# A residual block with three MLPs: the norm's roots ahead of the last two MLPs taken per token column and spread by matmuls

## The reference

```python
def _rmsnorm(x, g):
    xf = x.astype(jnp.float32)
    y = xf * lax.rsqrt(jnp.mean(xf * xf, axis=-1, keepdims=True) + RMS_EPS)
    return (y * g.astype(jnp.float32)).astype(x.dtype)

def _sqrelu_mlp(h, w_up, w_down):
    a = jax.nn.relu(jnp.einsum('bld,df->blf', h, w_up))
    return jnp.einsum('blf,fd->bld', a * a, w_down)

    for i in range(DEPTH_2):
        ...
        h = _rmsnorm(hres, norm_g[i, 2])
        hres = hres + _rmsnorm(_sqrelu_mlp(h, w_up[i], w_down[i]), norm_g[i, 3])
```

## Time and profile before

| | |
|---|---|
| time, median of 3 runs | 2014.34 us (2013.67 to 2019.06) |
| the profiled execution | 2016.18 us, of it a span of 2014.4 us from first to last instruction |
| PE busy | 1916.4 us (95%) |
| DVE busy | 1278.6 us (63%) |
| ACT busy | 785.0 us (39%) |
| mean granted TensorE clock | 0.975 of full speed |

### The profile page before, as it was taken

The page is one execution under the profiler, slowest core; times in us unless marked ns, Lnnn a source line. Parts: engine busy times, 40 slices in busy tenths (PEclk is TensorE's granted clock), DMA queues, the critical chain, the costliest instruction groups (busy, mean ns, idle before and its releaser), DMA issues.

```text
span 2014.4 us, 28679 instructions
## 1 busy us (share of the span) xinstructions
PE 1916.4 (95%) x11702; PEld 1690.6 (84%) x11702; DVE 1278.6 (63%) x1912; ACT 785.0 (39%) x1180; POOL 156.3 (8%) x127
## 2 busy tenths in 40 slices
PE   7999899999999899999988999999899988999996
PEld 6876777888888778989888999999899866898995
DVE  7676646434434776766658677776655467777774
ACT  4555434222213343443334444443422244444441
POOL 3000033000000220000011000000300130000001
PEclk9999999999999999999998999999899988999998
DMA  5130121223232131111121233233122311332321
GB/s 178 63 105 21 53 84 63 101 88 105 84 105 104 64 104 63 43 43 43 64 81 46 84 105 105 84 106 105 54 93 85 105 63 63 105 105 86 107 101 42
DMA packets 26077, 166.44 MB, mean 83 GB/s; under 512 B 3808, under 2 KB 4064, under 8 KB 6624
## 3 DMA queue, kind: packets, MB, share of 16 engines
q1 hardware_dynamic: 25232, 163.52, 23.7%
q10 hardware_dynamic: 720, 1.14, 0.2%
HBM read 162.55 MB, written 2.10 MB: 82 GB/s over the span
## 4 chain that ended last, share of the span: by engine, by line
PE 42%; DVE 7%; ACT 1%; issue 1%; ACTq 0%; DVEq 0%
PE ps L2515 6%; PE ps L2516 6%; PE ps L2517 6%; PE ps L2531 4%; PE ps L2530 4%; PE ps L2529 4%; PE ps L372 3%; PE ps L374 3%; PE ps L373 3%; DVE ps L529 1%; DVE h L542 1%; DVE z_lo L480 1%; DVE w_lo L354 1%; ACT w_hi L343 0%; DVE arena L1885 0%
## 5 line engine op out<-in xcount | busy, mean ns | idle before, releaser
L372 PE MATMUL ps<-z_hi,w_hi 128*128 128x512 f32 (+1 forms) x1008 | 368.4, 365 | 30.6 <-DVE z_lo L480 27.5
L373 PE MATMUL ps<-z_lo,w_hi 128*128 128x512 f32 (+1 forms) x1008 | 364.3, 361 | 0.0
L374 PE MATMUL ps<-z_hi,w_lo 128*128 128x512 f32 (+1 forms) x1008 | 363.0, 360 | 0.0
L354 DVE TENSOR_TENSOR w_lo<-w_raw,w_hi 128x2048 fp32r<-128x2048 f32 x95 | 217.7, 2292 | 97.9 <-ACT w_hi L343 97.8
L2515 PE MATMUL ps<-arena,w_hi 128*128 128x256 f32 (+2 forms) x768 | 249.8, 325 | 17.6 <-DVE acc L1848 8.8
L372 PEld LDWEIGHTS ps<-z_hi,w_hi 128*128 128x128 f32 x1008 | 195.0, 193 | 67.9 <-issue 22.8
L2516 PE MATMUL ps<-arena,w_hi 128*128 128x256 f32 (+2 forms) x768 | 249.5, 325 | 0.0
L2517 PE MATMUL ps<-arena,w_lo 128*128 128x256 f32 (+2 forms) x768 | 248.9, 324 | 0.0
L343 ACT ACTIVATE w_hi<-w_raw 128x2048 fp32r<-128x2048 f32 x95 | 180.9, 1904 | 144.4 <-PE ps L374 131.6
L374 PEld LDWEIGHTS ps<-z_hi,w_lo 128*128 128x128 f32 x1008 | 194.8, 193 | 29.8
L373 PEld LDWEIGHTS ps<-z_lo,w_hi 128*128 128x128 f32 x1008 | 195.3, 194 | 28.8 <-issue 0.7
(11 more groups left out here) (357 smaller groups left out, 4145.7 us busy)
## 6 DMA issues: line engine op xcount, KB each, us to landing
w_raw<-wstream SPq DMA_DIRECT2D x151, 1024.0 KB, 4.8
out<-h SPq DMA_DIRECT2D x8, 256.0 KB, 2.0
w_raw<-wstream SPq DMA_DIRECT2D x2, 512.0 KB, 6.1
h<-xT ACTq DMA_DIRECT2D x4, 256.0 KB, 6.5
h<-xT SPq DMA_DIRECT2D x4, 256.0 KB, 6.3
rope_cs<-pT SPq DMA_DIRECT2D x1, 512.0 KB, 5.6
acc<-pos SPq DMA_DIRECT2D x1, 256.0 KB, 10.4
acc<-lam SPq DMA_DIRECT2D x1, 128.0 KB, 9.8
```

Source lines behind the costliest of these rows:

```text
L354: dve.tensor_tensor(w_lo[:, slot, :], w_raw[:, slot, :], w_hi[:, slot, :].bitcast(f32), ALU.subtract).then_inc(wlo, 1)
L372: pe.matmul(dst, wh, zh, start=(k == 0), stop=False)
L373: pe.matmul(dst, wh, zl, start=False, stop=False)
L374: last = pe.matmul(dst, wl, zh, start=False, stop=(k == nk - 1))
```

## The change

Ahead of the second and the third MLP, the root and the reciprocal are taken per column, of 128 x 6 or 128 x 4 numbers in `cols` in place of 128 x 514 or 128 x 512 in `rr`. The second up block carries two insertions. After two of its steps PE makes the columns. After eight of its steps (`second_at` = 8) it waits for the reciprocal (`rstd`) and spreads the columns to free PSUM. ACT then copies the spread numbers from PSUM to `rr`, in one piece (512 tokens) or in three (514), and `plain(0)` waits for that copy (`r_home`) and no longer for `rstd`. The other norms are as before.

```diff
-        def project(pe, wslot, slot, first_tile, nk, z, ntok, before, z_ready=None, by_tile=False, middle=None, middle_at=2, home=None):
+        def project(pe, wslot, slot, first_tile, nk, z, ntok, before, z_ready=None, by_tile=False, middle=None, middle_at=2, home=None,
+                    second=None, second_at=8):
...
+                if second is not None and n == second_at:
+                    second()
...
+        def r_pieces(slot, ntok):
+
+            b = 4 * slot
+            if ntok <= 512:
+                return [(i, ps[:, b + 1, P * i:P * i + P]) for i in range(4)]
+            return [(0, ps[:, b, 0:P]), (1, ps[:, b, P:2 * P]), (3, ps[:, b + 2, 0:P]), (4, ps[:, b + 2, P:2 * P]),
+                    (5, ps[:, b + 1, 258:258 + P])]
+
+        def r_parts(slot, ntok):
+
+            b = 4 * slot
+            if ntok <= 512:
+                return [(0, ntok, ps[:, b + 1, 0:ntok])]
+            return [(0, 256, ps[:, b, 0:256]), (256, 512, ps[:, b + 2, 0:256]), (512, 514, ps[:, b + 1, 384:386])]
+
+        def column_home(slot, ntok):
+
+            return ps[:, 4 * slot + (ntok <= 512), 0:len(starts(ntok))]
+
+        def pe_r_columns(pe, si, slot, ntok, c0):
+
+            pe.wait_ge(summed, summed_to(si))
+            pe_columns(pe, column_home(slot, ntok), [ssum[:, c0:c0 + ntok]], ntok).then_inc(stat, 1)
+
+        def pe_r_spread(pe, si, slot, ntok):
+
+            pe.wait_ge(rstd, si + 1)
+            for i, dst in r_pieces(slot, ntok):
+                last = pe.matmul(dst, cols[:, U_COL + i:U_COL + i + 1].to_broadcast([P, P]), ident[:, :], start=True, stop=True)
+            last.then_inc(s("r_spread"), 1)
+
+        def act_r_root(act, si, slot, ntok):
+            act.wait_ge(stat, si + 1)
+            act.activation(cols[:, U_COL:U_COL + len(starts(ntok))], column_home(slot, ntok), ACT.Sqrt, bias=eps[:, 0:1],
+                           scale=1.0 / D).then_inc(rooted, 1)
+
+        def dve_r(dve, si, ntok):
+            dve.wait_ge(rooted, si + 1)
+            dst = cols[:, U_COL:U_COL + len(starts(ntok))]
+            dve.reciprocal(dst, dst).then_inc(rstd, 1)
+
+        def act_r_home(act, n, slot, ntok, c0):
+            act.wait_ge(s("r_spread"), since("r_spread", n))
+            for a, b, src in r_parts(slot, ntok):
+                last = act.activation(rr[:, 0, c0 + a:c0 + b], src, ACT.Copy)
+            last.then_inc(s("r_home"), 1)
...
-                act_root(act, si, p0 % 2, ntok, T - ntok)
+                act_r_root(act, si, p0 % 2, ntok)
+                act_r_home(act, l + 1, p0 % 2, ntok, T - ntok)
...
-                dve_rstd(dve, si, ntok, T - ntok)
-                dve.wait_ge(rstd, si + 1)
+                dve_r(dve, si, ntok)
+                dve.wait_ge(s("r_home"), since("r_home", l + 1))
                 plain(0)
...
-                up_plain(1, middle=lambda: pe_stat(pe, si, p0 % 2, ntok, T - ntok))
+                up_plain(1, middle=lambda: pe_r_columns(pe, si, p0 % 2, ntok, T - ntok), second=lambda: pe_r_spread(pe, si, p0 % 2, ntok))
```

More of the change, by code:

```diff
@@ L264, in build @@
                    "us_y": ("m_d", 16), "us_x": ("m_e", 28), "t_sum": ("m_p", 16), "t_hi": ("m_hi", 4), "t_lo": ("m_lo", 4),
-                   "t_part": ("c_norm", 3), "dh_hi": ("c_hi", 3), "dh_lo": ("c_lo", 3)}
+                   "t_part": ("c_norm", 3), "dh_hi": ("c_hi", 3), "dh_lo": ("c_lo", 3),
+                   "r_spread": ("c_spread", 2), "r_home": ("c_rcp", 1)}
         def since(name, n):
@@ L419, in pe_spread @@
             return last
+        U_COL = 111
+        def r_pieces(slot, ntok):
[32 more added lines that the diff above has]
+            last.then_inc(s("r_home"), 1)
         def pe_post_stat(pe, pi, ntok, c0):
```

## The result

| | before | changed |
|---|---|---|
| median | 2014.53 us (20 runs, 2012.82 to 2019.07) | 2018.39 us (20 runs, 2015.57 to 2022.37) |
| profiled execution | 2016.18 us, span 2014.4 us | 2017.32 us, span 2015.2 us |

The ratio of the changed kernel to the one before is 1.0016, with a 95% interval of 1.0009 to 1.0023: 3.2 us slower (1.8 to 4.6). So the change costs a little, and it is within the 0.3% that were named as no difference. On the page, PE is busy for 1913.0 us (1916.4 before) and the DVE for 1273.7 us (1278.6 before). For the DVE that is less work. For PE it isn't, since the spreads have come on top; but the mean granted clock was 0.979 in this execution and 0.975 in the one before, so less of PE's work ran at half clock.

A forecast was written before the change was run, and what follows sets the result against it. The DVE was taken to bound the kernel through the start of `plain(0)`; delays of 1.71 us (second MLP) and 0.49 us (third) sum to +2.2 us, so 2014.34 + 2.2 = 2016.5 us, range 2013.0 to 2020.1.

The forecast's parts named there:

- What bounds: Second and third MLP: the DVE's queue sets PE's two stalls, so a shift of `plain(0)`'s start moves the kernel's end equally.
- (a): Column sums on PE in the second up block: twelve records take 1.37 us (second MLP), eight 0.91 us (third).
- (b): Small root, then small DVE reciprocal behind the weight block's low part: done near 1078.8 us (second MLP), 1653.8 (third).
- (c): PE reaches the spread after 36 matmuls, 4.36 us (second MLP), or 18, 4.18 us (third); its queue place binds.
- (d): PE's spread of the columns: ten records take 1.28 us in the second MLP, eight 1.06 us in the third.
- (e): ACT's copies, priced as roots: 0.99 and 0.69 us; `plain(0)` then starts 1.71 us (second MLP) and 0.49 us (third) later.
- The stalls: PE's waits ahead of the first down block: first ones become 3.9 and 4.1 us, second ones stay as they are.
- The rival of 2027.3 us: Second up block at half clock from the columns on, slowing matmuls and spreads: +13.0 us; chance 0.06.
- The rule of the Trainium skill: Read alone, `plain(0)` follows the small reciprocal at once and the full 6.4 us is gained: 2007.9 us; chance 0.03.

## Why the prediction held

The forecast was 2016.5 us in a range of 2013.0 to 2020.1, within 0.3% of before and a little slower; measured were 2018.39 us and 3.2 us more than before. Step by step:

- **What bounds.** Held. The short reciprocal on the kernel before gave 7.5 us where the chain promised 6.4, and a spread at two other places moved the time as the start of `plain(0)` moved.
- **(a) The columns.** A little too dear. From their start to the start of the next matmul twelve records took 1.26 us and eight 0.81, for 1.37 and 0.91 forecast.
- **(b), (c) The place in PE's queue is last.** Held: 2.45 us between the reciprocal's end and the spread's start, for 2.5 forecast, and no wait of PE.
- **(d) The spread.** 1.28 us in the second MLP and 1.05 us in the third, for 1.28 and 1.06.
- **(e) ACT's copies.** Too large. They were priced as the roots, 0.99 and 0.69 us, and took 0.72 and 0.60, which is 0.09 us less for each piece. With these 0.27 and 0.09 us less, and with the spread reached 0.12 and 0.02 us sooner after the start of the columns, the delay is 1.32 and 0.38 us by the distance from the low part, for 1.71 and 0.49 forecast: 1.7 us in sum, for 2.2. The waits of the DVE are as much shorter than forecast, 4.52 and 3.59 us for 4.9 and 3.7.
- **The stalls.** The first were given as 3.9 and 4.1 us and are 3.7 and 4.0. The second were to "stay as they are", 4.0 and 4.8 us; they are 5.1 and 5.2. What failed there is the assumption that PE spends the same time on the first two tiles between the stalls. It took 8.6 us before (1102.09 to 1110.65) and 7.5 us now (1100.55 to 1108.04 by the waits), since less of it was at half clock, and in the third MLP 7.8 and 7.4 us. As the DVE sets the end of the stall, that difference is lost in waiting.
- **The clock in the second up block.** The rival of 2027.3 us is excluded: 1.00 with columns and spreads in it.

What stays open is the difference between the 1.7 us that the two traces show at `plain(0)` and the 3.2 us (1.8 to 4.6) of the medians. It may be no more than the interval's width. More time at half clock in the changed kernel would be another reason, and the runs don't bear it out: the mean granted clock of its 20 executions is 0.9775, and that of the 41 executions of the kernel before in the two series of experiments is 0.9764. So the terms of the sum held within 0.5 us in all, and 1.5 of the 3.2 us measured are in none of them.

The rule of the Trainium skill, "Perfetto Trace Analysis", "Optimization Strategies", to speed up the engine that blocks the critical path, was neither wrong nor enough here. The two reciprocals did become shorter by 6.4 us; the operand came later by more. With the gap filled the rule's value came out in full, 7.1 us (4.4 to 9.7).

## What to carry to other kernels

When a long step on the bounding engine is replaced by a short one and a round trip over other engines, count the round trip from the place that each step has in the queue of its engine, not from the data it needs: here 36 matmuls (18 in the third MLP) stood between the columns and the spreads, each of about a microsecond. The idle time that such a round trip leaves on the bounding engine is worth as much as the work that can be moved into it, so look for steps that need nothing of it before trying to shorten the trip. And when an engine in order holds up another, look at what each stall ends at: the place of two DVE copies of 0.6 us, behind steps that PE wasn't waiting for then, was worth 13.7 us, more than the short reciprocals with their gap filled.

## What was not expected of the hardware

A copy on ACT from PSUM took 0.60 us for 128 x 512, where a root of the same shape took 0.69 us, and 0.72 us for three pieces (256, 256 and 2 columns) where three roots (256, 254 and 4) took 0.99. Both differences come to 0.09 us a piece. The roots read a bias from a tile (`eps`) and the copies don't; that this is the reason is not tested by any run.

The time of one and the same kernel goes with the mean clock that it was granted. Of the 20 executions of the changed kernel, the two at a clock of 0.975 took 2022.2 us on average, the five at 0.978 took 2018.2 and the one at 0.980 took 2015.6, about 1.2 us for each 0.001 by a line through all 20. In the 41 executions of the kernel before it is 0.7 us for each 0.001, with more scatter. So most of the 7 us between the fastest and the slowest run of the changed kernel goes with the clock, and is not noise of the measurement; that the clock is the cause, and what moves it from one execution to the next, is not shown.
